# Expert overflow in 32-token blocks with an early loop exit, and a second weight buffer set moved from the down units to four gate-and-up units

## The reference

```python
counts = jnp.bincount(flat_e, length=N_EXPERTS)      # tokens of each expert, 1024 in all
def expert_block(args):
    tok, e = args
    xb = xt_pad[tok]
    gate, up = jnp.split(xb @ w_gu[e] + b_gu[e], 2, axis=-1)
    gate = jnp.minimum(gate, SWIGLU_LIMIT)
    up = jnp.clip(up, -SWIGLU_LIMIT, SWIGLU_LIMIT)
    act = (up + 1) * (gate * jax.nn.sigmoid(SWIGLU_ALPHA * gate))
    return act @ w_dn[e] + b_dn[e]
y = jnp.zeros((T + 1, D), jnp.float32).at[slot_tok].add(yb * slot_w[:, None])
```

## Time and profile before

| | us |
|---|---|
| median of three runs | 2116.4 (2112.89 to 2121.94) |
| the profiled execution, its own time | 2111.71 |
| its span | 2110.0 |
| expert stage on PE, first bias matmul to last down matmul | 362.6 to 1383.0 |
| PE busy over the span | 1948.9 (92%) |
| DVE, ACT, POOL busy | 908.0, 469.5, 70.5 |
| HBM read | 579.23 MB, of which 402.65 MB are expert weights |

### The profile page before, as it was taken

How to read it: one execution, slowest core, us unless ns; L and a number is a source line. 1 busy time by engine, 2 the same in 40 slices (tenths; PEclk the granted TensorE clock), 3 DMA queues, 4 the chain that set the end, 5 groups by cost and what they waited for, 6 DMA issues and landing times. The chain is left out here.

```text
span 2110.0 us, 28553 instructions
## 1 busy us (share of the span) xinstructions
PE 1948.9 (92%) x10917; PEld 1222.1 (58%) x10918; DVE 908.0 (43%) x1444; ACT 469.5 (22%) x557; POOL 70.5 (3%) x128
## 2 busy tenths in 40 slices
PE   4999896999999999999999999989999998999998
PEld 2859774433333333333333333358987997878986
DVE  3799644111111111111111121176556787876554
ACT  2223101000000000100000000024543643334542
POOL 2000002000000000000000000010000000020000
PEclk9999997999999999999999999999999989999999
DMA  9794834959999999899999985936555620054552
GB/s 360 246 324 156 300 126 146 417 216 422 421 422 422 422 422 422 332 423 422 422 422 422 408 344 226 401 107 213 180 198 164 202 96 1 1 173 162 189 190 80
DMA packets 143604, 581.37 MB, mean 276 GB/s; under 512 B 10520, under 2 KB 12552, under 8 KB 94281
## 3 DMA queue, kind: packets, MB, share of 16 engines
q1 hardware_dynamic: 136384, 564.43, 68.6%
q0 software_dynamic: 3040, 11.02, 1.7%
q10 hardware_dynamic: 4105, 4.86, 0.7%
HBM read 579.23 MB, written 1.05 MB: 275 GB/s over the span
## 5 line engine op out<-in xcount | busy, mean ns | idle before, releaser
L1182 PE MATMUL bank<-ring,area 128*64 128x512 f32 x2048 | 459.2, 597 | 28.0 <-DMA ring<-in_w_gu 27.6
L1182 PEld LDWEIGHTS bank<-ring,area 128*64 128x64 f32 x2048 | 144.0, 137 | 325.3 <-issue 235.5
L924 PE MATMUL bank<-area_r,ring_r 128*128 128x256 f32 x992 | 282.6, 285 | 9.3 <-DVE area_r L2155 7.1
L926 PE MATMUL bank<-area_r,ring_r 128*128 128x256 f32 x992 | 281.5, 284 | 0.0
L927 PE MATMUL bank<-area_r,ring_r 128*128 128x256 f32 x992 | 281.5, 284 | 0.0
L289 DVE TENSOR_TENSOR ring_r<-ring,ring_r 128x2048 fp32r<-128x2048 f32 x90 | 205.8, 2291 | 149.8 <-ACT ring_r L286 148.1
L2420 DVE TENSOR_SCALAR area<-bank 128x512 f32<-128x512 f32 x36 | 24.9, 692 | 539.6 <-PE bank L1182 539.6
L286 ACT ACTIVATE ring_r<-ring 128x2048 fp32r<-128x2048 f32 x92 | 175.7, 1913 | 179.4 <-PE bank L927 152.2
L924 PEld LDWEIGHTS bank<-area_r,ring_r 128*128 128x128 f32 x992 | 191.3, 193 | 12.1 <-DVE area_r L2155 7.3
L1220 PE MATMUL bank<-area 128*64 128x512 f32 x864 | 192.5, 594 | 0.6 <-DVE area L2434 0.5
L926 PEld LDWEIGHTS bank<-area_r,ring_r 128*128 128x128 f32 x992 | 191.3, 193 | 0.0
(11 more groups left out here) (341 smaller groups left out, 2177.8 us busy)
## 6 DMA issues: line engine op xcount, KB each, us to landing
ring<-in_w_gu SPq DMA_DIRECT2D x256, 1024.0 KB, 21.1
area<-in_w_dn SPq DMA_DIRECT2D x96, 1024.0 KB, 21.0
ring<-in_mlp_w SPq DMA_DIRECT2D x64, 1024.0 KB, 5.4
ring<-in_w_dn SPq DMA_DIRECT2D x32, 1024.0 KB, 19.5
ring<-in_w_in SPq DMA_DIRECT2D x24, 1024.0 KB, 6.3
ring<-in_gdn_w_in SPq DMA_DIRECT2D x16, 1024.0 KB, 5.5
area<-in_w_mod SPq DMA_DIRECT2D x12, 1024.0 KB, 8.6
ring<-in_w_mod SPq DMA_DIRECT2D x8, 1024.0 KB, 17.1
```

The lines of the kernel that those rows point to most:

```text
L924: ins = mm(out_, a_[0], b_[0], start=start, stop=False)
L926: mm(out_, a_[0], b_[1], start=False, stop=False)
L1182: ins = mm(bk[hf * BLK:(hf + 1) * BLK, :], x(kt), block_u[:, c:c + BANK], start=False, stop=kt == ND - 1)
```

## The change

The edit has three parts.

The overflow block shrinks from 64 to 32 tokens (`OBLK`). All four quarters of an overflow block's gate and up go to the four 32-column quarters of PE and land in one bank (`over_gate_and_up`); down puts its two output halves, and the two halves of its contraction, into four quarters too, whose sum is taken by the scatter through a fourfold spread matrix (`over_down`). Rows handled by DVE and ACT are 64 partitions instead of 128, with the same number of columns, except for the token copy, whose 512 columns become 256. The two transposed halves of the activations go to one bank and are copied by one instruction. An expert with 65 to 96 tokens runs one such block, one with 97 to 128 tokens runs two.

The inner loop becomes a loop that starts at block 2 (of 32 tokens) and ends at the first empty one. Overflow steps get semaphores of their own (`over_pe`, `over_dve`, `over_act`) and a count of blocks done in a register, so empty blocks have nothing to add. PE now ends an overflow block by waiting until ACT has copied its result.

The second buffer set belongs to gate-and-up units 4 to 7, and the down units have one slot each. Loads are issued in the order in which slots come free: units 0 to 3 of an expert, units 4 to 7 of the next one, units 8 to 11 of the first, and so on.

```diff
-        GU_SLOTS = tuple(range(NGU))
-        DN_SLOTS = ((8, 9, 10, 11), (12, 13, 14, 15))
+        TWICE = (4, 5, 6, 7)
+        ONCE_SLOTS = {0: 0, 1: 1, 2: 2, 3: 3, 8: 4, 9: 5, 10: 6, 11: 7}
+        TWICE_SLOTS = ((8, 9, 10, 11), (12, 13, 14, 15))
...
-        load_order = [(0, u) for u in range(NGU)] + [(0, u) for u in range(NGU, NU)]
-        for e in range(1, NE):
-            load_order += [(e, u) for u in range(NGU, NU)] + [(e, u) for u in range(NGU)]
+        def ahead_of_use(x):
+            e, u = x
+            return use_order(e, u) - (NU if u in TWICE else 0)
+
+        load_order = sorted(((0, u) for u in range(NU)), key=lambda x: expert_slot(*x)) + \
+            sorted(((e, u) for e in range(1, NE) for u in range(NU)), key=ahead_of_use)
...
                 if n >= ER:
-                    sp.wait_ge(w_used, PRE + n - ER + 1)
+                    sp.wait_ge(w_used, PRE + use_order(e - (EG if u in TWICE else 1), u) + 1)
...
-                    with eng.Fori(1, NBLK) as b:
-                        with eng.If(n_tok - b * BLK > 0):
-                            overflow((g, j, b))
+                    nc.regs_mov(at_block, OVER0)
+                    nc.br(turn, engines=me)
+                    with nc.body(turn, valid_engines=me):
+                        b = nc.snap(at_block, min_val=OVER0, max_val=OVER1 - 1)
+                        with eng.If(n_tok - b * OBLK > 0):
+                            overflow((g, j, (b, nc.snap(blocks_done, min_val=0, max_val=S))))
+                            nc.regs_alu(blocks_done, blocks_done, 1, op=ALU.add)
                         with eng.Else():
 
-                            steps.started(eng, (g, j, b))
-                            eng.sem_inc(steps.sem, steps.over_len)
+                            nc.regs_mov(at_block, OVER1)
+                        nc.regs_alu(at_block, at_block, 1, op=ALU.add)
+                        nc.br_lt(at_block, OVER1, on_true=turn, on_false=f"{turn}_end", engines=me)
...
+            def over_gate_and_up(w):
+
+                for kt in range(ND):
+                    block_u = weights(w, kt)
+                    for q in range(4):
+                        ins = mm(bG[q * OBLK:(q + 1) * OBLK, :], xg_o[:, kt, :], block_u[:, q * BANK:(q + 1) * BANK],
+                                 start=False, stop=kt == ND - 1)
+                step(ins, w[2])
...
+            def over_down(w):
+
+                DV.did(pe, w, "act_T")
+                for n, v in enumerate(DN_ORDER):
+                    fh, i = v // 2, v % 2
+                    block_u = weights(w, NGU + n)
+                    for k in range(2):
+                        for hf in range(2):
+                            r, c = (2 * hf + k) * OBLK, k * D + hf * BANK
+                            ins = mm(bT[r:r + OBLK, :], over_T[:, 2 * i + k, fh * OBLK:(fh + 1) * OBLK],
+                                     block_u[:, c:c + BANK], start=n == 0, stop=n == 3)
+                step(ins, w[2])
...
             def overflow(w):
                 DV.did(pe, w, "slots1")
                 AC.started(pe, w, less=1)
-                gather(slots_o)
-                gate_up_bias()
+                over_gather(w)
+                over_bias()
                 DV.did(pe, w, "tokens")
-                gate_and_up(w, lambda kt: xg_o[:, kt, :], False)
+                over_gate_and_up(w)
                 AC.started(pe, w)
-                scatter(spread_T, y_blk)
+                scatter(spread_T, y_blk, b=w[2])
                 spread_transposed(w, spread)
-                activation_T(w, 0, bG)
-                activation_T(w, 1, bU)
-                down(w, False)
+                over_activation_T(w)
+                over_down(w)
+                AC.did(pe, w, "down")
```

More of the change, by code:

```diff
@@ L580, in build, with __init__ @@
         class Steps:
[L584 to L588, removed]
-                self.main = [{n: overs + i + 1 for i, n in enumerate(m)} for m in mains]
+            def __init__(self, sem_, over_sem, mains, over, base):
+                self.sem, self.over_sem, self.base, self.over_len = sem_, over_sem, base, len(over)
+                self.first = [sum(len(m) for m in mains[:j]) for j in range(EG)]
+                self.per = sum(len(m) for m in mains)
+                self.main = [{n: i + 1 for i, n in enumerate(m)} for m in mains]
                 self.over = {n: i + 1 for i, n in enumerate(over)}
@@ L594, in did @@
                 g, j, b = where
-                base = self.base + self.first[j] - pairs_ago * self.per
                 if isinstance(b, int):
+                    base = self.base + self.first[j] - pairs_ago * self.per
                     eng.wait_ge(self.sem, g * self.per + (base + self.main[j][step]))
                 else:
-                    eng.wait_ge(self.sem, g * self.per + b * self.over_len + (base - self.over_len + self.over[step]))
+                    _, blocks = b
+                    eng.wait_ge(self.over_sem, blocks * self.over_len + self.over[step])
@@ L601, in started @@
             def started(self, eng, where, less=0):
-                g, j, b = where
-                base = self.base + self.first[j] - less
-                if isinstance(b, int):
-                    eng.wait_ge(self.sem, g * self.per + (base + (NBLK - 1) * self.over_len))
-                else:
-                    eng.wait_ge(self.sem, g * self.per + b * self.over_len + (base - self.over_len))
-        PE = Steps(moe_pe, (PE_MAIN, PE_MAIN), PE_OVER, 3)
-        DV = Steps(moe_dve, (DVE_FIRST, DVE_MAIN), DVE_OVER, 2)
@@ L612, in build, with step @@
-        AC = Steps(moe_act, (ACT_FIRST, ACT_SECOND), ACT_OVER, 3)
+                g, j, _ = where
+                eng.wait_ge(self.sem, g * self.per + (self.base + self.first[j] - less))
+            def step(self, ins, b):
+                ins.then_inc(self.sem if isinstance(b, int) else self.over_sem, 1)
+        PE = Steps(moe_pe, over_pe, (PE_MAIN, PE_MAIN), PE_OVER, 3)
+        DV = Steps(moe_dve, over_dve, (DVE_FIRST, DVE_MAIN), DVE_OVER, 2)
+        AC = Steps(moe_act, over_act, (ACT_FIRST, ACT_SECOND), ACT_OVER, 3)
@@ L1208, in spread_transposed, with down @@
                              start=True, stop=True)
-                step(ins)
-            def down(w, last):
+                step(ins, w[2])
+            def down(w):
                 for n, v in enumerate(DN_ORDER):
@@ L1282, in last_block @@
                 spread_transposed(w, spread)
-                down(w, True)
+                down(w)
             pe.wait_ge(moe_act, 3)
```

147 lines of the change are left out of this document (87 added, 60 removed).

## The result

The changed kernel took 2121.17 us (median of 20 runs, 2118.98 to 2126.85) against 2116.11 us (20 runs, 2108.22 to 2121.94) of the kernel before. The ratio is 1.0029 [1.0021, 1.0038], which is 6.1 us slower; the two medians are 5.1 apart. The forecast was 3.8 us faster. Both lie within the 0.5% that I called no change, and the time lies inside the range; but the direction was wrong, and the interval excludes the forecast. The profiled execution took 2120.71 us with a span of 2119.0 (before: 2111.71 and 2110.0).

The account below looks back on a forecast made before the run. The expert stage was taken to run at the weight stream's pace up to expert 27, then PE's. Changes of -10.0 (expert 2), +18.7 (16), -2.5 (27) and -10.0 (29) gave -3.8 us: 2112.6 us, range 2104 to 2122.

Parts of the forecast that it names:

- Four blocks of 31.05 become five of 21.0: Overflow blocks: one each at experts 2, 27 and 29, two at 16; alone 124 us against 105.
- rival (c): Small block: four quarters do not run side by side, block 31.3 us, +32 us, 2148 in all; chance 0.05.
- The forecast's own sign of being wrong, gate and up above 8 us: Small block's gate and up, forecast at 6.88 us; above 8 us would show the forecast wrong.
- X32 = 21.0 us: Length of one 32-token overflow block, summed from gather to way out; 10.0 us less than the 64-token block.
- F + 4.5: Experts 16 and 27: held first block ends 4.5 us after F, when the weight stream stops for full slots.
- The way out: End of a small block: 0.69 us for ACT's copy plus 1.2 for branches, taken between 0.8 and 1.6.
- rival (d): New loop's branches stop PE 1.8 us or more per block and per expert; +10.6 us, 2127; chance 0.08.
- The load order, 2.3 us at each held block, nothing otherwise: New load order costs 2.3 us at experts 16 and 27, where down units arrive last, and gives nothing back.
- about 6 was forecast: Expert 16's first small block: PE waits about 6 us for down weights.
- F + 2.2: Experts 16 and 27 with the old load order: block held by gate and up ends 2.2 us after F.
- as a whole: Stages behind the expert stage keep their instructions and move as a whole, at no cost or gain.
- Two blocks at expert 16: Expert 16, 99 tokens: held first block plus a second of 21.0 us; change +18.7 us, running total +8.7.

Follow-up runs that it names:

- e4: Changed kernel, its overflow gather streaming the same 32 columns twice, 64 in all; 2120.51 us, ratio 1.0013 to the kernel before.
- e7: Changed kernel, PE waiting for ACT's copy only ahead of the next gather or scatter, not at the block's end; 2103.58 us, ratio 0.9951.
- e2: Kernel before with the new slots and load order alone, 64-token blocks and old loop kept; 2117.79 us, ratio 1.0005.
- mended pair: Changed kernel with late wait and 64-column gather, timed on one chip with the old load order (2091.21 us) and the new (2099.17 us).
- e1: Changed kernel with the slots, load order and load wait of the kernel before; 2114.49 us, ratio 0.9997.
- e5: Changed kernel without the second overflow block of expert 16, three tokens' results missing; 2092.98 us, ratio 0.9890.
- e6: Changed kernel with four extra full-width matmuls into a free bank ahead of each small block's down; 2129.82 us, ratio 1.0066.
- e10: Changed kernel with the late wait and the old slots and load order, gather kept at 32 columns; 2100.18 us, ratio 0.9933.
- e8: Changed kernel with the late wait, the 64-column gather and the old slots and load order together; 2092.44 us, ratio 0.9886.
- e12: e8's kernel timed again, beside the one that differs by the new slots alone, on one chip; 2091.21 us, ratio 0.9886.
- e11: Kernel before with the new early-exit loop and the late wait, 64-token blocks and old slots kept; 2104.56 us, ratio 0.9948.
- e3: Kernel before with the early-exit loop, separate semaphores and PE's wait for ACT's copy, 64-token blocks and old slots; 2113.28 us, ratio 0.9984.

## Why the prediction was right in its steps and wrong in its sum

**Four blocks of 31.05 become five of 21.0.** Right in number and at full clock in size: 21.41 and 21.29 us where the clock held (e4). Four quarters ran side by side (3.64 us for down's 32 records), so rival (c) fell; gate and up of the small block took 7.0 us (e4, 419.48 to 426.48), with 6.88 forecast. The forecast's own sign of being wrong, gate and up above 8 us, did come in the changed kernel, with 8.3 us at expert 2 and 9.5 in the second block of expert 16; it pointed not at the quarters but at the clock.

**The step that failed is the sum's unspoken one: X32 = 21.0 us at each block that is not held, and F + 4.5 at each that is, with each term from a row at full clock.** The text names the clock nowhere. The small block changed what every PE row of before had in common, that PE was busy around it. Measured in its place: the second block of expert 16 took 25.96 us instead of 21.0 (gather 2.1 of it, gate and up 2.6, way out 0.3), expert 29's 24.25, the held first block ended at F + 6.1 (1.91 instead of about 1.1 us for the last unit, 0.7 for a later landing), and main blocks behind overflows were up to 1.7 us longer. 6.5 at expert 16, 3.2 at 29 and 1.1 ahead of it are 10.8 us, as much as the miss of 10.7 in the table. The later landing and the two ways out are 1.2 to 1.3 of it; the rest, some 9.6 us, is half clock. That the clock did this is shown by the rows' own granted clock, by the twin gathers of 3.76 and 5.86 us, and by e4 and e7, which changed what PE does ahead of a stretch and gave the full-clock durations back. At expert 2 half clock cost some 1.3 us too (22.75 against e4's 21.41); it doesn't show in the sum because the gain ahead of that block, which the forecast had at nothing as well, is larger. Without this piece of luck the miss would be bigger.

**The way out** was 1.2 behind a copy of 0.69 in the forecast, 1.89 in all; from ACT's start to the bias it was 2.06 to 2.25, within its bounds. But its price was more than its length. It left PE idle, and e7 gave back 16.5 us, by ratios from two chips, where five ways out of 2.2 are 11. Branches fetched nothing: both instruction queues moved the same packets as before (54 and 21), so rival (d)'s cause was absent. The rule beside it, that a taken branch to a target outside the two pages held forces a fetch (the Trainium skill, Runtime: NRT & Kernel Launch, Instruction fetch mechanics), had nothing to act on here. Of the control-flow prices that I weighed (the Trainium skill, Advanced Engine Details and Errata, Control Flow Timing) the rows are again far above: some 1.5 us behind the copy, for the branches, their register work and PE's restart, against 0.3, the estimate from that page's figures.

**The load order, 2.3 us at each held block, nothing otherwise.** Where it acts in the stage was right (e2: nothing with long blocks), and so was that PE waits for down weights (4.45 and 4.28 us, where about 6 was forecast). The term itself holds at full clock: in the mended pair the hold at expert 16 costs 2.2 us, and the first blocks end at F + 0.5 and F + 2.9, where the forecast's F + 2.2 and F + 4.5, less the 1.89 of the way out that these kernels do not have, are 0.3 and 2.6. In the changed kernel and e1 they end at F + 6.1 and F + 2.1, 4.0 us apart; 0.8 of that is the last unit at half clock and 0.7 its later landing. The total was off: about 7 us in the changed kernel, 8.0 in the mended one, where 4.6 was forecast. In the mended pair's traces the rest is half clock at and behind expert 27 (some 1.6 of the 6.1 at the stage's end) and what lies behind the stage, which the forecast moved "as a whole": the idle of 1.3 us that every kernel with the new order shows there, and a drop of the clock whose link with the order is not shown. The profiled spans are 2.2 further apart than the timed medians, so this split is good to some 2 us.

**Two blocks at expert 16** were named as the reason why the total moves little. e5 puts the second at 29 us where the forecast's terms make it 21.0; with that block gone the changed kernel is 1.1% faster than before.

**What stays open.** Which idle on PE brings the clock down: e6 filled the longest gap and did not keep it up; e10 shows a narrow gather with and without a drop; e2 has drops at experts without any overflow; and the same kernel (e8 and e12) has a drop at expert 16 in one profile and none in the other. In e12, PE waits 1.42 us for every 1.06 of work from 844 to 850, at full clock; in e8 and e10 the clock fell in the middle of the same waits. No condition fits all of these, and I give none.

The best version is e8's kernel, confirmed as e12: 32-token blocks, early exit, late wait, wide gather, old load order, 1.14% faster than the kernel before (24 us). Of that the early exit with the late wait is 0.5% (e11), and the smaller block with its wide gather the rest, some 13 us, compared over two chips. No run has the small block in the old loop.

## What to carry to other kernels

When a change shortens a block or adds a wait on PE, price the block at both clock levels that its rows can have, and look at what now stands idle ahead of it: here half clock cost some 9.6 us, more than the gain that the forecast had left. A wait at the end of a block drains the engine and lays bare the branches behind it; the same wait ahead of the first instruction that needs it cost 0.24 us or nothing. Before halving a block, count the data: 99 tokens against a limit of 96 cost 29 us. Where a block holds the whole ring of buffers, its own units should stand ahead of the next expert's in the load order; here its down units came last, and the block could not end before them. And price a hold against the moment at which the stream stops, not by the length of the block, which also grows when PE merely arrives earlier.

## What the runs showed of the hardware that I had not expected

PE's granted clock fell to 0.50 in stretches of 3 to 14 us in the middle of a stage with PE busy 93% of the time, behind waits of 2 to 4.5 us, and sometimes behind a gather of 128x32 matmuls with no wait at all; twice the columns in that gather took no more time (3.79 and 3.81 us), and the clock stayed up through the blocks of experts 2 and 29. A way out with 2.2 us of idle was followed by half clock in some passes (877 and 1218 in e3) and not in others (at 448 the bias took its 0.62 us).
